# Encoder trunk on one core: in the differential attention, both distance products of a head before its score products, and the score products alternating between the two maps

## The chip, the cores and the metric

The kernel runs on one core of a Trainium2 chip. The metric is the device time of one execution in microseconds (us), the median of several runs. The other engines named below are TensorE (PE in the profile; its weight loads are listed apart as PEld), VectorE (DVE), ScalarE (ACT), GpSimd (POOL) and the queue that issues DMAs (SP).

## The reference, cut to what matters

Two layers of an encoder for 256 positions of width 1024. The part that the change touches is the attention with two score maps per head:

```
# q, k: (B,S,H,2,dh), H = 8 heads, 2 maps, dh = 64
sc = jnp.einsum('bqhcd,bkhcd->bhcqk', qi, k)
dist = jnp.abs(qpos[:, None] - kpos[None, :])
sc = sc - slopes[None, :, None, None, None] * dist
p = jax.nn.softmax(sc, axis=-1)
attn = p[:, :, 0] - lam * p[:, :, 1]
```

Each layer also has a cross-attention, a state-space branch, gates, three branch projections and a feed-forward part; the projections are the bulk of the work.

## The kernel before

All weights are streamed from memory in units of 128x1024 values into a ring of four slots. For each unit ScalarE rounds the raw values to a high part (`wH`, line 921) and VectorE or GpSimd takes the rest as a low part (`wL`, lines 1312 and 1240). TensorE multiplies by three products (high by high, high by low, low by high) into one of two large accumulators `PS`. `unit` (line 609 is the helper `mm` that issues each product) is the stream of the large products, 440 units for both layers.

Everything else is a side step, placed by hand between units by the table of `layer_plan`. On TensorE a step stands after the unit of its number; for head h of the differential attention the steps are `da_scores` (the products of this change), then `da_max` (VectorE, line 1484), `da_exp` (ScalarE, line 1071, which also writes the slope tile of head h+2, line 1009), `da_combine`, `da_turn`, `da_copy`, `da_values` and `da_head`, and `da_scores` of the next head comes three units after that of the one before it. There are 8 heads in each of 2 layers, so `da_scores` runs 16 times.

Map m of a head accumulates in its own bank, `S0` for map 0 and `S1` for map 1 (each 128x512: two blocks of 128 queries by 256 keys). First comes the distance product in bf16 (a diagonal tile of slopes by `dist`, 128 rows deep, 512 columns), then two fp32 score products, one for each block of queries, added onto it. A head has 64 dimensions in each map, and `qT` and `kT` (both in `regB`) hold map 0 in partitions 0 to 63 and map 1 in partitions 64 to 127, so a score product is 64 rows deep. `take(lay, m)` waits until bank m was released by its last reader (`side_free`). For heads 1 to 7 that is `da_exp` of the head before, whose second of four exponentials releases bank 0 and whose fourth bank 1.

Of the kernel before, what the change touches and what calls it, by code (L numbers as in the profile page):

```python
# [39 lines left out]
NT = T // P  # L40
# [3 lines left out]
HEADS, HALF = 8, 4  # L44
DH = 64
# [224 lines left out]
def build(nc, x, mem, mix_norm_g, w_in, lq1, lk1, lq2, lk2, subln_g, conv_w, conv_b, dt_bias, A_log, D_skip,  # L270
# [3 lines left out]
    with ctx:  # L274
# [3 lines left out]
        def sem(name):  # L278
            return ctx.enter_context(nc.semaphore(name))
# [138 lines left out]
        slope_ready = sem("slope_ready")  # L418
# [181 lines left out]
        def _(pe):  # L600
            side = [0, 0, 0, 0]

            def take(lay, bank):

                pe.wait_ge(side_free[bank], lay * side_uses[bank] + side[bank] + 1)
                side[bank] += 1

            def mm(o, l, r, first, last):
                return nc.tensor.matmul(o, l, r, start=first, stop=last, skip_group_check=True)  # L609
# [113 lines left out]
            def step(lay, kind, i):  # L723
# [48 lines left out]
                elif kind == "da_scores":  # L772
# [2 lines left out]
                        wait_evacuated(pe, lay, "k", half)  # L775
                    for m in range(2):
                        take(lay, m)
                        if m == 0:
                            pe.wait_ge(slope_ready, HEADS * lay + i + 1)
                        mm(S[m][:, :], slopes[:, P * (i % 2):P * (i % 2 + 1)], dist[:, :], True, False)  # L780
                        r = slice(DH * m, DH * (m + 1))
                        for t in range(NT):
                            ins = mm(S[m][:, T * t:T * (t + 1)], qT[half][r, j, P * t:P * (t + 1)],
                                     kT[half][r, j, :], False, True)
                    ins.then_inc(da_sc, 1)
# [28 lines left out]
                elif kind == "xs_turn":  # L814
                    bank = XS_BANK[i]
                    take(lay, bank)
                    n, t = i // 2 + 2, i % 2
# [77 lines left out]
            for lay in range(DEPTH):  # L895
                side[:] = setup_side
                each_step("pe", lambda u, g, c: unit(lay, u, g, c), lambda g: None, lambda *s: step(lay, *s),
                          lambda g: ffn_units(lay, g))
                counted = [n - m for n, m in zip(side, setup_side)]
# [840 lines left out]
```

## Time and profile before

| | |
|---|---|
| time, median of 3 runs | 1439.89 us (1439.86 to 1440.32) |
| span of the profiled execution, first to last instruction | 1438.7 us |
| TensorE busy | 1417.2 us, 99% of the span |
| VectorE / ScalarE / GpSimd busy | 65% / 61% / 23% |
| DMA, mean rate | 178 GB/s |
| granted TensorE clock, mean | 0.998 of full speed |

The profiled execution gives its span; its own time is not listed apart. The median is 1.2 us above the span, which is what lies around the first and the last instruction. Busy time says how long an engine had work in it, not whether the work was dense. An fp32 product appears as two matmul records with a weight load each, an fp32r or bf16 product as one. The record of the first distance product of a head is missing from the trace (16 of 32 are there), but its weight load is recorded.

### The profile page before, as it was taken

What the parts mean: (1) busy time and instruction counts of PE and PEld (TensorE: products, weight loads), DVE (VectorE), ACT (ScalarE), POOL (GpSimd) and SP (SyncE); (2) the same over time, 40 slices, a digit from 0 to 9 for tenths busy, and PEclk for the clock granted to TensorE, in tenths of its full rate; (3) what the DMA queues carried; (4) which work ended last, traced back from release to release, by engine and by line L of the source; (5) the groups of instructions that cost most, each with busy time, mean ns of one, the idle gap of its engine ahead of it and who ended that gap; (6) DMA issues with size and microseconds to landing.
All of it is one profiled execution on the core that took longest, in us unless ns stands there. A gap on an engine that the chain in (4) does not pass through costs nothing.

```text
span 1438.7 us, 25282 instructions
## 1 busy us (share of the span) xinstructions
PE 1417.2 (99%) x8861; PEld 1266.6 (88%) x8877; DVE 937.6 (65%) x1223; ACT 876.4 (61%) x1408; POOL 337.1 (23%) x161
## 2 busy tenths in 40 slices
PE   7999999999999999999999999999999999999997
PEld 7899888888888889998899998988888888999986
DVE  5478475787998446554444764668889875565543
ACT  7576667886755455445466665678777464544453
POOL 0410000010023344444423000001110244354442
PEclk9999999999999999999999999999999999999999
DMA  7655445475665655556555554454777556555664
GB/s 247 191 174 162 131 119 148 141 215 195 210 191 177 189 177 162 177 183 239 179 179 180 163 162 119 140 172 124 221 190 227 170 176 190 162 176 180 195 225 146
DMA packets 158496, 255.48 MB, mean 178 GB/s; under 512 B 12729, under 2 KB 58923, under 8 KB 158379
## 3 DMA queue, kind: packets, MB, share of 16 engines
q1 hardware_dynamic: 157819, 252.84, 57.4%
q8 instruction: 61, 1.00, 0.3%
q10 hardware_dynamic: 560, 1.18, 0.2%
q14 instruction: 56, 0.46, 0.1%
HBM read 252.80 MB, written 1.18 MB: 177 GB/s over the span
## 4 chain that ended last, share of the span: by engine, by line
PE 98%; ACT 1%; DVE 0%; DMA 0%; DVEq 0%; issue 0%; ACTq 0%; SPq 0%
PE PS L609 85%; PE S L609 9%; PE S L616 1%; PE S L820 0%; PE S L885 0%; PE S L791 0%; DMA regA<-in_mem_dram 0%; PE S L761 0%; PE S L811 0%; ACT regB L996 0%; DVE wL L1312 0%; DVEq L1388 0%; ACT hH L1003 0%; ACT wH L921 0%; ACTq L998 0%
## 5 line engine op out<-in xcount | busy, mean ns | idle before, releaser
L921 ACT CAST wH<-w_raw 128x1024 fp32r<-128x1024 f32 x443 | 457.5, 1042 | 427.2 <-PE PS L609 374.4
L1312 DVE TENSOR_TENSOR wL<-w_raw,wH 128x1024 fp32r<-128x1024 f32 (+1 forms) x331 | 459.5, 1393 | 355.3 <-ACT wH L921 333.8
L1240 POOL TENSOR_TENSOR wL<-w_raw,wH 128x1024 fp32r<-128x1024 f32 (+1 forms) x112 | 285.5, 2550 | 409.7 <-ACT wH L921 409.6
L609 PE MATMUL PS<-hH,wH 128*128 128x256 f32 (+1 forms) x1488 | 370.9, 287 | 0.0
L609 PE MATMUL PS<-hL,wH 128*128 128x256 f32 (+1 forms) x1488 | 365.2, 283 | 0.0
L609 PEld LDWEIGHTS PS<-hH,wH 128*128 128x128 f32 (+1 forms) x1488 | 283.9, 191 | 3.3 <-issue 2.7
L609 PEld LDWEIGHTS PS<-hL,wH 128*128 128x128 f32 (+1 forms) x1488 | 284.2, 191 | 0.6
L609 PE MATMUL PS<-wH,actH 128*128 128x512 f32 x560 | 223.9, 400 | 0.0
L609 PE MATMUL PS<-wH,actL 128*128 128x512 f32 x560 | 218.5, 390 | 0.0
L609 PE MATMUL PS<-hH,wL 128*128 128x256 f32 (+1 forms) x1488 | 211.0, 283 | 0.0
L609 PEld LDWEIGHTS PS<-hH,wL 128*128 128x128 f32 (+1 forms) x1488 | 192.0, 191 | 0.0
L609 PE MATMUL PS<-wH,hH 128*128 128x512 f32 x384 | 159.1, 414 | 0.0
L609 PE MATMUL PS<-wH,hL 128*128 128x512 f32 x384 | 150.4, 392 | 0.0
L609 PE MATMUL PS<-wL,actH 128*128 128x512 f32 x560 | 150.0, 390 | 0.0
L609 PEld LDWEIGHTS PS<-wL,actH 128*128 128x128 f32 x560 | 105.1, 188 | 22.4
L609 PEld LDWEIGHTS PS<-wH,actH 128*128 128x128 f32 x560 | 105.3, 188 | 22.2 <-issue 1.4
L609 PEld LDWEIGHTS PS<-wH,actL 128*128 128x128 f32 x560 | 105.3, 188 | 22.1 <-issue 1.4
L609 PE MATMUL PS<-wL,hH 128*128 128x512 f32 x384 | 103.2, 390 | 0.0
L609 PEld LDWEIGHTS PS<-wH,hH 128*128 128x128 f32 x384 | 72.2, 188 | 17.8 <-issue 4.6
L1267 POOL TENSOR_TENSOR scr<-actHf,dts 128x512 f32<-128x512 f32 x16 | 20.6, 1285 | 284.2 <-PE S L791 223.8
L609 PEld LDWEIGHTS PS<-wL,hH 128*128 128x128 f32 x384 | 72.1, 188 | 15.9
L609 PEld LDWEIGHTS PS<-wH,hL 128*128 128x128 f32 x384 | 72.3, 188 | 15.4 <-issue 1.9
(237 smaller groups left out, 1533.5 us busy)
## 6 DMA issues: line engine op xcount, KB each, us to landing
w_raw<-in_w_in_dram SPq DMA_DIRECT2D x192, 512.0 KB
w_raw<-in_w_ffn_in_dram SPq DMA_DIRECT2D x176, 256.0 KB
w_raw<-in_w_branch_dram SPq DMA_DIRECT2D x64, 512.0 KB
w_raw<-in_w_ffn_out_dram SPq DMA_DIRECT2D x44, 512.0 KB
w_raw<-in_w_mem_kv_dram SPq DMA_DIRECT2D x35, 512.0 KB
regA<-cs_rows SPq DMA_DIRECT2D x64, 256.0 KB, 4.7
w_raw<-in_w_out_dram SPq DMA_DIRECT2D x16, 512.0 KB
regA<-in_mem_dram SPq DMA_DIRECT2D x6, 512.0 KB, 4.8
```

Source lines behind the costliest of these rows:

```text
L609: return nc.tensor.matmul(o, l, r, start=first, stop=last, skip_group_check=True)
L616: ins = nc.tensor.transpose(dst[:, at:at + P], src(t, k), ident[:, :])
L921: nc.scalar.copy(wH[:, slot].rearrange("p k c -> p (k c)")[:, q], raw[:, slot].rearrange("p k c -> p (k c)")[:, q]).then_inc(h_done[slot], 1)
L1240: nc.gpsimd.tensor_tensor(wL[:, slot].rearrange("p k c -> p (k c)")[:, q], raw[:, slot].rearrange("p k c -> p (k c)")[:, q], wH[:, slot].r ...
L1267: nc.gpsimd.tensor_tensor(v3(xsd[i % 2], HPG), v3(xsN[g][:, c, :], HPG), dgain[:, SH * c + HPG * g:SH * c + HPG * (g + 1)].unsqueeze(2) .b ...
L1312: v.tensor_tensor(wL[:, slot].rearrange("p k c -> p (k c)")[:, q], raw[:, slot].rearrange("p k c -> p (k c)")[:, q], wH[:, slot].rearrange ...
```

## The change

Only `da_scores` changes. Both banks are taken first, then the slope tile is waited for; both distance products are issued one behind the other; then the four score products follow in the order block 0 of map 0, block 0 of map 1, block 1 of map 0, block 1 of map 1.

```
--- before
+++ after
                     for m in range(2):
                         take(lay, m)
-                        if m == 0:
-                            pe.wait_ge(slope_ready, HEADS * lay + i + 1)
+                    pe.wait_ge(slope_ready, HEADS * lay + i + 1)
+                    for m in range(2):
                         mm(S[m][:, :], slopes[:, P * (i % 2):P * (i % 2 + 1)], dist[:, :], True, False)
-                        r = slice(DH * m, DH * (m + 1))
-                        for t in range(NT):
+                    for t in range(NT):
+                        for m in range(2):
+                            r = slice(DH * m, DH * (m + 1))
                             ins = mm(S[m][:, T * t:T * (t + 1)], qT[half][r, j, P * t:P * (t + 1)],
                                      kT[half][r, j, :], False, True)
                     ins.then_inc(da_sc, 1)
```

The order of instructions on TensorE at head 0 of layer 0, before. `S0` and `S1` are the banks of the maps, `dist,slopes` is the distance product, `regB` a score product (two matmul records each), `PS0` the large accumulator:

```order
L609 MATMUL PS0<-wL,hH 128x512 x3
L609 MATMUL S0<-dist,slopes 128x512 [waits slope_ready,side_free0,psum_free1]
L609 MATMUL S0<-regB 128x256 x2
L609 MATMUL S1<-dist,slopes 128x512 [waits side_free1]
L609 MATMUL S1<-regB 128x256 x2
L609 MATMUL PS0<-wH,hH 128x512 [waits h_done1]
```

The same place in the changed kernel:

```order
L609 MATMUL PS0<-wL,hH 128x512 x3
L609 MATMUL S0<-dist,slopes 128x512 [waits side_free1,slope_ready,side_free0,psum_free1]
L609 MATMUL S1<-dist,slopes 128x512
L609 MATMUL S0<-regB 128x256
L609 MATMUL S1<-regB 128x256
L609 MATMUL S0<-regB 128x256
L609 MATMUL S1<-regB 128x256
L609 MATMUL PS0<-wH,hH 128x512 [waits h_done1]
```

The distance product of map 1 has moved ahead of the score products of map 0, its wait for `side_free1` has moved to the first distance product, and map 0 and map 1 now take turns. The number and the shapes of the products are the same.

Head 2 of layer 0 on TensorE, before, where the fp32 values product of another head stands directly ahead:

```order
L609 MATMUL S2<-regB,scr 128x128 x3
L609 MATMUL S0<-dist,slopes 128x512 [waits slope_ready,side_free0]
L609 MATMUL S0<-regB 128x256 x2
L609 MATMUL S1<-dist,slopes 128x512 [waits side_free1]
L609 MATMUL S1<-regB 128x256 x2
L609 MATMUL PS0<-hH,wH 128x256 [waits h_done3]
```

And in the changed kernel:

```order
L609 MATMUL S2<-regB,scr 128x128 x3
L609 MATMUL S0<-dist,slopes 128x512 [waits slope_ready,side_free1,side_free0]
L609 MATMUL S1<-dist,slopes 128x512
L609 MATMUL S0<-regB 128x256
L609 MATMUL S1<-regB 128x256
L609 MATMUL S0<-regB 128x256
L609 MATMUL S1<-regB 128x256
L609 MATMUL PS0<-hH,wH 128x256 [waits h_done3]
```

The neighbours on both sides are unchanged here too. The other engines keep their order.

## Rows read from the trace of the kernel before

**Rows 1.** The page: span, busy time, TensorE clock in 40 slices, chain that ended last.
```profile
span 1438.7 us, 25282 instructions
PE 1417.2 (99%) x8861; PEld 1266.6 (88%) x8877; DVE 937.6 (65%) x1223; ACT 876.4 (61%) x1408; POOL 337.1 (23%) x161
PEclk9999999999999999999999999999999999999999
PE 98%; ACT 1%; DVE 0%; DMA 0%; DVEq 0%; issue 0%; ACTq 0%; SPq 0%
```

**Rows 2.** The table of waits on TensorE, whole span.
```profile
engine line waited for: us in total, times, longest us
PE PS L629 <- DMA regB<-in_da_subln_g_dram: 7.6, 1, 7.6
PE S L616 <- DVEq L1388: 1.1, 2, 0.5
PE S L609 <- issue: 1.0, 6, 0.2
PE S L616 <- DVEq L1344: 1.0, 1, 1.0
PE PS L609 <- issue: 0.2, 1, 0.2
```

**Rows 3.** The timeline of head 0, layer 0, weight loads and matmuls.
```profile
start us, us, engine line op out<-in xcount [idle before <-releaser]
168.49 0.10 PEld L609 LDWEIGHTS S<-dist,slopes 128*128 128x128 bf16 x1 [0.26 <-issue]
168.81 1.13 PE L609 MATMUL S<-regB 64*128 64x256 f32 x4 [0.16 <-issue]
169.87 0.10 PEld L609 LDWEIGHTS S<-dist,slopes 128*128 128x128 bf16 x1 [0.33 <-issue]
170.19 1.13 PE L609 MATMUL S<-regB 64*128 64x256 f32 x4
171.25 0.19 PEld L609 LDWEIGHTS PS<-wH,hH 128*128 128x128 f32 x1 [0.33 <-issue]
171.35 0.19 PEld L609 LDWEIGHTS PS<-wH,hL 128*128 128x128 f32 x1
171.58 0.39 PE L609 MATMUL PS<-wH,hL 128*128 128x512 f32 x1
171.59 0.19 PEld L609 LDWEIGHTS PS<-wH,hH 128*128 128x128 f32 x1
171.81 0.39 PE L609 MATMUL PS<-wH,hH 128*128 128x512 f32 x1
171.82 0.19 PEld L609 LDWEIGHTS PS<-wH,hL 128*128 128x128 f32 x1
```

**Rows 4.** Durations of the score matmuls and of the distance products, all heads.
```profile
engine op xcount: duration ns min/median/max, first and last start us, forms
L609 PE MATMUL S<-regB x128: 376/376/480, 168.8 to 980.6; 64*128 64x256 f32 x128
L609 PEld LDWEIGHTS S<-dist,slopes x32: 95/96/100, 168.5 to 979.5; 128*128 128x128 bf16 x32
```

**Rows 5.** The timeline around the only other products 64 rows deep (line 828).
```profile
69.12 0.52 PE L609 MATMUL PS<-hH,wL 128*128 128x256 f32 x3
69.57 0.33 PE L828 MATMUL S<-ident,scr 64*128 64x64 f32 x2
70.06 0.28 PE L609 MATMUL PS<-hL,wH 128*128 128x256 f32 x1
70.17 0.28 PE L609 MATMUL PS<-hH,wH 128*128 128x256 f32 x1
```

**Rows 6.** The timeline of head 2: its first distance load directly behind a values product.
```profile
193.73 0.83 PE L609 MATMUL S<-regB,scr 128*128 128x128 f32 x6
194.29 0.10 PEld L609 LDWEIGHTS S<-dist,slopes 128*128 128x128 bf16 x1
194.71 1.13 PE L609 MATMUL S<-regB 64*128 64x256 f32 x4
```

**Rows 7.** The timeline ahead of head 5: last exponential of head 4, and the first distance load.
```profile
241.86 0.48 ACT L1071 ACTIVATE scr<-S,small 128x256 f32<-128x256 f32 x1
242.31 0.32 ACT L1009 ACTIVATE slopes<-ident 128x128 bf16<-128x128 f32 x1
243.60 0.10 PEld L609 LDWEIGHTS S<-dist,slopes 128*128 128x128 bf16 x1
```

**Rows 8.** Busy time of the engines in the two stretches that hold all heads.
```profile
core 0: us, PE busy (x) PEld busy (x) DVE busy (x) ACT busy (x) POOL busy (x), PEclk, DMA share, GB/s
168.00:280.00 112.00, 110.78 (x702) 95.79 (x709) 69.99 (x114) 76.39 (x178) 1.05 (x1) 1.00 0.49 142
876.00:988.00 112.00, 110.78 (x703) 95.89 (x710) 70.35 (x114) 76.61 (x179) 1.05 (x1) 1.00 0.48 142
```

**Rows 9.** The tables of waits of ScalarE, VectorE and the DMA queue, 160 to 280 us.
```profile
ACT wH L921 <- PE PS L609: 31.5, 14, 4.6
DVE wL L1312 <- ACT wH L921: 40.6, 20, 5.1
DVE small L1484 <- PE S L609: 2.9, 5, 0.9
SPq L532 <- DVE wL L1312: 87.7, 27, 5.5
```

## The prediction

> **What bounds the kernel now.** I read the page first, then the waits of TensorE, then single instructions around one head. The page shows TensorE busy for 1417.2 of 1438.7 us and 98% of the chain that ended last, with the clock at full speed (the 2.4 GHz level) in every slice [rows 1]. Busy could still hide gaps, so the waits come next: TensorE waits 7.6 us for the first DMA and after that 3.3 us in all, none of it at a distance or score product for another engine [rows 2]. The others wait for TensorE. In the first stretch with heads ScalarE's rounding waits 31.5 us for products to release ring slots, VectorE waits 40.6 us for the rounding, and the DMA queue 87.7 us for slots [rows 9]; VectorE is busy for 70 and ScalarE for 76 of 112 us [rows 8]. So a nanosecond taken out of TensorE's stream is a nanosecond of the kernel, until some step is late.
>
> **What a head costs now.** In head 0 the first distance load starts at 168.49, the score matmuls of map 0 at 168.81, the second distance load at 169.87, the score matmuls of map 1 at 170.19, and the next large product's load at 171.25 [rows 3]. So a map is a distance block of 0.32 and a score block of 1.06, and a head 2.76 us; 16 heads are 44 us, 3.1% of the span.
>
> The score block taken apart: four matmul records end 1.13 after their first start; the first lasts 0.480, the others 0.376 [rows 3, 4]. The 0.104 between them is a weight load that nothing hides. The last record starts 1.13 - 0.376 = 0.754 after the first, so the pitch is (0.754 - 0.104)/3 = 0.217. From the last start to the next load 1.06 - 0.754 = 0.306 pass: one pitch, and 0.089 in which nothing is issued. This is the crossing from products 64 rows deep to ones 128 rows deep. The distance block tells the other direction: 0.323 less 0.089 leaves 0.234, which is near the 0.23 between two large products of 512 columns (171.58, 171.81) [rows 3]. A third place with 64 rows confirms it: the three matmuls at 69.12 have a pitch of (0.52 - 0.28)/2 = 0.12 and would be through at 69.48, but the 64-row one starts at 69.57, 0.09 later [rows 5].
>
> **The change, part by part.**
>
> 1. *Crossings.* A head crosses four times now (128 to 64 and back, twice), afterwards twice. Removed are two idle pieces of 0.089 and one naked weight load of 0.104, the one behind the second crossing into 64 rows: 0.282 a head. Nothing else ran on TensorE in them, and nothing hides them. Over 16 heads 4.5 us.
>
> 2. *The second distance product behind the first.* The trace has no two bf16 products in a row. From below its load is hidden, and the block costs a pitch of about 0.213 (0.234 less the 0.02 that the load at 168.49 seems to cost), a gain of 0.02. From above the whole load record of 0.096 is naked [rows 4], 0.31 in place of 0.234, a loss of 0.07. In head 2 the bf16 load directly behind an fp32 product started at once, before that product was through [rows 6]. I take 0.234 as now, thus zero, and keep +0.3 and -1.2 us for the whole kernel as bounds.
>
> 3. *Alternating halves.* The eight score passes of a head (four products, two records each) now run A1 A2 B1 B2 A3 A4 B3 B4, A in partitions 0 to 63 and bank S0, B in 64 to 127 and bank S1. In series they cost 8 x 0.217 = 1.74. No row shows two neighbouring products in different halves, so I bound it from both sides. At best B1 runs beside A2, A3 beside B2 and B3 beside A4: five slots in place of eight, 3 x 0.217 = 0.65 a head, 10.4 us in all. At worst each of the three changes of half costs what a crossing costs with its naked load, 0.089 + 0.104 = 0.193, so 0.58 a head or 9.3 us lost.
> Between them I go by how weight loads stand to matmuls. Every load in the stream starts with the start of the matmul ahead of it and not sooner: 171.58 and 171.59, 171.81 and 171.82 [rows 3]. If that order holds when the half changes, the load of B1 starts with A2, takes 0.107 (its 0.104 and issue), and B1 then need not wait for A2 to end. B1 starts 0.107 after A2 in place of 0.217: 0.11 saved at each of three changes, 0.33 a head, 5.3 us in all. I take this value. It is nearest to the rows, which show loads in order and one matmul ahead, and it needs only that the halves can work at once. That they are treated as parts of their own is suggested by the idle 0.089 at every crossing, which equal shapes do not have.
> The Trainium skill (TensorE: Matmul & The Clock Gate, Part 3: Packing small matmuls) says that matmuls in different row groups run at the same time, with starts about 4 ns apart, and that weight loads are pulled ahead when the row group differs. By that rule the sum would take the whole 10.4 us of five slots; no row here shows it.
>
> 4. *The moved wait.* Bank 1 is now needed at the first distance product, 1.38 us earlier (169.87 less 168.49) [rows 3]. The closest head is head 5: the fourth exponential of head 4 ends at 241.86 + 0.48 = 242.34, and the head starts at 243.60 [rows 7]. 1.26 us are left, so the wait costs nothing; without that cover it would cost what it is late, with the whole large stream queued behind it. The units between two heads take as long as before, so this distance does not shrink with the change itself. The slope tile was written two heads ago.
>
> 5. *Who sees the end of the head.* The maxima on VectorE wait for the last score product (2.9 us in 5 waits [rows 9]) and simply start sooner. Nothing is added on any other engine or queue.
>
> The sum: 4.5 + 0 + 5.3 + 0 = 9.8 us. The profiled span is 1438.7, and 1.2 us lie around it; against the median of 1439.89 this gives 1430.1 us, 0.7% faster.
>
> **The rivals.**
>
> - *Full overlap of the halves.* Loads may run two matmuls ahead when their half is free. For it speaks that the gap between loads is long enough (0.107 of each 0.217); against it that no load in the rows ever starts that early. 4.5 + 10.4 = 14.9 us, 1425.0 us.
> - *No overlap: the change does not do what it says.* The passes stay in line at 0.217 and only the crossings are saved: 1435.4 us. For it speaks that every row has matmuls at the pitch of their columns, with 64 rows or with 128.
> - *A change of half costs like a crossing.* Three of 0.193 against 0.282 saved make a head 0.30 longer, 4.8 us in all: 1444.7 us. It decides from 0.094 a change, and is measurable from about 0.15. For it speaks that the engine does go idle when the depth changes, against it that the depth here stays at 64.
> - *The gain is taken back.* A weight unit or a side step becomes late when TensorE is 0.6 us faster per head: 1438 to 1440 us. Against it speak the waits of all others for TensorE [rows 8, 9].
>
> **How the numbers follow.** Half overlap 0.36, full overlap 0.27, no overlap 0.22, change of half as dear as a crossing 0.07, taken back 0.05, and 0.03 for something outside. The predicted time is that of the first, 1430.1. The range takes in the first three with the bounds of item 2: from 1424.5 to 1436.2; within the likeliest case alone it would be 1429 to 1432. A measurement of this kernel can tell about 0.2%, 2.9 us, from no change; even the case without overlap lies 4.5 us below. Faster 0.88, same 0.05, slower 0.07.
>
> **What would show it.** Between the first distance load of a head and the next large load: 2.15 us for my case, 1.83 for full overlap, 2.48 for none, 3.06 if a change of half costs like a crossing, where 2.76 stand now. The score records should be eight in one block, with one first record of 0.48. In my case the starts inside the block would alternate between steps of 0.22 and of 0.11; in the rival of full overlap some starts would be nearly together. The idle 0.089 should be there 32 times in place of 64. I would be wrong if ScalarE's last exponential stood directly ahead of a head, if TensorE showed waits on rounding in these stretches, or if the second distance block came out far from 0.23.

## The result and the profile after

The changed kernel takes 1424.21 us (1424.01 to 1424.59), against 1439.99 us for the kernel before in the same rounds: a ratio of 0.989, 95% interval 0.988 to 0.990, 15.8 us less. The time lies 0.3 us under the low end of the forecast range and 5.9 us under the predicted 1430.1. It was clearly faster, but by 15.8 us where 9.8 were forecast.

The page of the changed kernel, lines of the span, the busy times and the chain that ended last:

```profile
span 1422.9 us, 25302 instructions
PE 1402.7 (99%) x8877; PEld 1256.5 (88%) x8877; DVE 936.0 (66%) x1223; ACT 876.6 (62%) x1408; POOL 337.8 (24%) x161
PE 91%; ACT 3%; DVE 2%; DVEq 1%; issue 1%; ACTq 1%; DMA 0%; SPq 0%
```

The span is 15.8 us shorter than in [rows 1]. TensorE's share of the chain fell from 98% to 91%; ScalarE and VectorE now have a part in it. The first is where the gain came from, the second is where some of it went.

The timeline of head 0 of layer 0 after the change, weight loads and matmuls:

```profile
168.61 0.12 PEld L609 LDWEIGHTS S<-dist,slopes 128*128 128x128 bf16 x2 [0.26 <-issue]
168.61 0.60 PE L609 MATMUL S<-dist,slopes 128*128 128x512 bf16 x2
169.15 0.73 PEld L609 LDWEIGHTS S<-regB 64*128 64x128 f32 x8 [0.42 <-issue]
169.15 1.13 PE L609 MATMUL S<-regB 64*128 64x256 f32 x8
170.21 0.50 PE L609 MATMUL PS<-wH,hH 128*128 128x512 f32 x1
```

Eight score matmuls take 1.13 us, exactly what four took in [rows 3]. A head is 170.21 - 168.61 = 1.60 us where it was 2.76. A head behind a values product gains the same: head 2 takes 1.69 us where it took 2.85 (before, its first distance load is at 194.29 and the next large load at 197.14; after, they are at 192.11 and 193.80). The start of the block seen through a narrow window, for both kinds of record:

```profile
169.15 0.19 PEld L609 LDWEIGHTS S<-regB 64*128 64x128 f32 x2 [0.42 <-issue]
169.15 0.49 PE L609 MATMUL S<-regB 64*128 64x256 f32 x2
```

Two matmuls, and two loads, start within 0.01 us of each other: one record lasts 0.480, the pair covers 0.49. A window up to 169.60 holds four:

```profile
169.15 0.70 PE L609 MATMUL S<-regB 64*128 64x256 f32 x4
```

So both passes of map 0 have a pass of map 1 beside them. It is not the second pass of one product beside the first of the next, as I had counted.

From the table of waits of TensorE in the changed kernel, the first DMA and the two lines that are new against [rows 2]:

```profile
PE PS L629 <- DMA regB<-in_da_subln_g_dram: 7.5, 1, 7.5
PE S L792 <- DVEq L1499: 0.8, 2, 0.4
PE S L609 <- ACT scr L1072: 0.6, 2, 0.3
```

The new ones are two places, once in each layer. Each is longer for the weight loads than for the matmuls, which run on for a while. The first place in layer 0, the weight load of a state-space product that writes bank `S0`, and the exponentials ahead of it:

```profile
246.26 0.47 ACT L1072 ACTIVATE scr<-S,small 128x256 f32<-128x256 f32 x1
246.86 0.19 PEld L609 LDWEIGHTS S<-regA 128*128 128x128 f32 x1 [0.54 <-ACT scr L1072]
```

The same two in the kernel before:

```profile
251.86 0.47 ACT L1071 ACTIVATE scr<-S,small 128x256 f32<-128x256 f32 x1
252.97 0.30 PEld L609 LDWEIGHTS S<-regA 128*128 128x128 f32 x2
```

The step is `cb` of group 0, which takes bank 0 after the exponentials of head 5. The second of them releases it. Before, it ended at 252.33, 0.64 us ahead of the load; now it ends at 246.73, the load follows 0.13 later, and TensorE's weight loads had stood still for half a microsecond (its matmuls for 0.30). The second place is the transposes of head 7:

```profile
277.74 0.88 DVE L1497 SCALAR_TENSOR_TENSOR scr<-scr,small 128x256 f32<-128x256 f32 x2
278.76 0.31 PEld L792 LDWEIGHTS S<-ident,scr 128*128 128x128 f32 x3 [0.80 <-issue]
```

They need what VectorE combines until 278.62. In the kernel before, the combination ended at 285.19 and the load came at 286.41, so there 1.22 us were in hand:

```profile
284.31 0.88 DVE L1496 SCALAR_TENSOR_TENSOR scr<-scr,small 128x256 f32<-128x256 f32 x2
286.41 0.14 PEld L791 LDWEIGHTS S<-ident,scr 128*128 128x128 f32 x1
```

### The profile page after: what moved, and what is told of

The parts are those of the page before. It is cut to its first block, busy times and chain, and to the rows that moved or that the text cites. A ratio compares the mean times of both kernels' runs of the same rounds, so it can differ in the third digit from the quotient of the medians.

```text
span 1422.9 us, 25302 instructions
## 1 busy us (share of the span) xinstructions
PE 1402.7 (99%) x8877; PEld 1256.5 (88%) x8877; DVE 936.0 (66%) x1223; ACT 876.6 (62%) x1408; POOL 337.8 (24%) x161
## 4 chain that ended last, share of the span: by engine, by line
PE 91%; ACT 3%; DVE 2%; DVEq 1%; issue 1%; ACTq 1%; DMA 0%; SPq 0%
PE PS L609 81%; PE S L609 7%; PE S L616 1%; DVE wL L1313 1%; ACT wH L922 1%; ACT scr L1072 1%; PE S L821 0%; PE S L886 0%; PE S L792 0%; DMA regA<-in_mem_dram 0%; DVEq L1486 0%; DVE actLf L1522 0%; ACT actLf L947 0%; PE S L761 0%; DVEq L1524 0%
## 5 line engine op out<-in xcount | busy, mean ns | idle before, releaser
L609 PEld LDWEIGHTS PS<-wL,hH 128*128 128x128 f32 x384 | 72.1, 188 | 15.8
```

## The experiments

The theory after the result: products in different halves of the rows run side by side in full, weight loads included, and this alone is most of the gain; the crossings are the rest; two late chains on VectorE took some back. Open were four things: whether the halves or something else did it, whether the alternation matters, how far a product may overtake, and whether the pauses can go.

### Both maps from one half

```
                             for m in range(2):
-                                r = slice(DH * m, DH * (m + 1))
+                                r = slice(0, DH)
```

> The order of the changed kernel, but both maps take their scores from the lower half of the partitions, so map 1 gets the scores of map 0 (the second map is not computed). If the different halves are what lets the products run together, the eight passes stand in line again: a head of 1.60 + 4 x 0.216 = 2.47 us, the kernel near 1435.3 us, and this is what the saved crossings alone are worth (4.6 us). If alternating banks alone did it, 1424 us as with the change.

Measured: 1435.22 us (1434.80 to 1435.82), ratio 0.997 (0.996 to 0.998). The timeline of its head 0:

```profile
167.79 0.12 PEld L609 LDWEIGHTS S<-dist,slopes 128*128 128x128 bf16 x2 [0.26 <-issue]
168.33 1.99 PE L609 MATMUL S<-regB 64*128 64x256 f32 x8
170.25 0.50 PE L609 MATMUL PS<-wH,hH 128*128 128x512 f32 x1
```

Shapes, banks and order are those of the change, and the eight matmuls take 1.99 us in place of 1.13. The head is 2.46. So it is the half of the rows that lets them run together, and alternating banks do nothing by themselves. The run also gives the worth of the other part of the change, the two crossings saved and the second distance product behind the first: 2.76 - 2.46 = 0.30 a head, 4.8 us in all, and the time is 4.74 us under that of the kernel before.

### Four crossings kept, one pair together

```
-                    for m in range(2):
-                        mm(S[m][:, :], slopes[:, P * (i % 2):P * (i % 2 + 1)], dist[:, :], True, False)
-                    for t in range(NT):
-                        for m in range(2):
+                    for what in ("d0", "00", "d1", "01", "10", "11"):
+                        if what[0] == "d":
+                            m = int(what[1])
+                            mm(S[m][:, :], slopes[:, P * (i % 2):P * (i % 2 + 1)], dist[:, :], True, False)
+                        else:
+                            m, t = int(what[0]), int(what[1])
                             r = slice(DH * m, DH * (m + 1))
```

> All four crossings kept: distance 0, one score product of map 0, distance 1, then the second of map 0, the first and the second of map 1. Overlap theory, in order: one pair runs together, two slots of 0.217 fewer than before, a head 2.33 us in place of 2.76, the kernel 1439.9 - 6.8 = 1433 us. If the gain came from having the distance products together, nothing: 1439.9 us.

Measured: 1433.16 us (1433.00 to 1434.12), ratio 0.995 (0.994 to 0.997), 6.80 us less. Its head 0:

```profile
168.32 0.70 PE L609 MATMUL S<-regB 64*128 64x256 f32 x2 [0.16 <-issue]
168.95 0.39 PE L609 MATMUL S<-dist,slopes 128*128 128x512 bf16 x1
169.27 1.13 PE L609 MATMUL S<-regB 64*128 64x256 f32 x6
```

Ahead of the second distance product two matmuls run alone; behind it six take the time of four. The two score products of map 1 stand behind that distance product, and the first score product of map 0 did not get one of them beside it. A distance product over all 128 rows acts as a barrier: nothing ran beside it, and no score product behind it was seen to pass it. This run alone does not show the second part, because in it two waiting products (distance 1 and the second of map 0) stand ahead of map 1, and two are not passed in any run (see below). The kernel before shows it: there only the distance product stands between the maps, and the scores of map 1 start behind it, at 170.19 [rows 3]. This is why the kernel before had no overlap at all. One rival stays open: in all these runs the distance product of map 1 writes the same bank as the scores of map 1, so no run tells whether its depth or its bank holds them back.

### The maps one after the other

```
-                    for t in range(NT):
-                        for m in range(2):
+                    for m in range(2):
+                        for t in range(NT):
```

> Both distance products first, but the score products in the old order (both blocks of map 0, then both of map 1). Theory 'in order, one product per half': a whole fp32 product (two passes) is issued when its half is free and the product ahead of it has been issued. Then only the second product of map 0 and the first of map 1 run together, six slots of 0.216 in place of four: a head from its first distance load to the next large load is 1.60 + 2 x 0.216 = 2.03 us, the kernel about 1429 us. Rival 'a queue for each half, any later product may overtake': four slots, 1.60 us, 1424 us. Rival 'no overlap unless they alternate': eight slots, 2.47 us, 1435.3 us.

Measured: 1424.08 us (1423.88 to 1424.31), ratio 0.989 (0.987 to 0.991), the same as the change. The in-order theory, for which I had 1429, falls. The rival has the right time; whether really any later product may overtake is the next question. A narrow window at the start of its score block:

```profile
168.47 0.20 PEld L609 LDWEIGHTS S<-regB 64*128 64x128 f32 x2 [0.42 <-issue]
168.47 0.49 PE L609 MATMUL S<-regB 64*128 64x256 f32 x2
```

Map 1 starts with map 0, though both products of map 0 stand ahead of it in the program. The alternation, half of the change, is worth nothing here. What matters is that no 128-row product stands between the maps: against the kernel before, this run only has the second distance product ahead of the scores of map 0.

### How far a product overtakes

Each score product is cut into two of 128 columns, so that each map has four, once map by map and once in turn.

```
-                    for t in range(NT):
-                        for m in range(2):
-                            r = slice(DH * m, DH * (m + 1))
-                            ins = mm(S[m][:, T * t:T * (t + 1)], qT[half][r, j, P * t:P * (t + 1)],
-                                     kT[half][r, j, :], False, True)
+                    for m in range(2):
+                        for t in range(NT):
+                            for k in range(2):
+                                r = slice(DH * m, DH * (m + 1))
+                                ins = mm(S[m][:, T * t + P * k:T * t + P * (k + 1)],
+                                         qT[half][r, j, P * t:P * (t + 1)],
+                                         kT[half][r, j, P * k:P * (k + 1)], False, True)
```

> The changed kernel with the score products map by map, and each cut into two of 128 columns: four products of map 0 stand ahead of the first of map 1. If the halves have queues that reach over all of them, map 1 still starts within some 20 ns of map 0, and a head is 1.6 to 1.8 us (eight passes of a half at a pitch of 0.11, with the loads at their limit of 0.107, instead of four of 0.216): 1424 to 1427 us. If only two products can be overtaken, map 1 starts two products, 0.44 us, later: a head of 2.05 us and more, 1431 us or more.

Measured: 1430.42 us (1430.35 to 1431.09), ratio 0.993 (0.992 to 0.995). A head takes 2.18 us. This is near the second case and far from the first: map 1 starts 0.55 us behind map 0 (168.15 and 168.70 in the rows below), where that case had 0.44.

```
-                    for m in range(2):
-                        for t in range(NT):
-                            for k in range(2):
+                    for t in range(NT):
+                        for k in range(2):
+                            for m in range(2):
```

> The products of 128 columns of e8_quarters, with the maps in turn. Theory: a half takes one product that runs and one that waits, and a product that finds its half full holds up everything behind it. With the maps in turn map 1 is then never held up: its first load comes within some 10 ns of that of map 0, and a head falls from 2.18 to 2.18 - 0.55 = 1.63 us if the loads of both halves can run side by side; the kernel 1424 to 1425 us. Rival: what made e8_quarters long is that weight loads of 0.107 in both halves share one path and 16 of them do not fit (16 x 0.107 = 1.7 us): a head stays at about 2.2 us and the kernel at 1430 us.

Measured: 1424.21 us (1423.85 to 1424.73), ratio 0.989 (0.987 to 0.991), a head 1.63 us, as the theory had it. The score blocks of head 0, first map by map, with a window that ends 0.54 us behind the start and one that begins right after it, then the whole block:

```profile
168.15 0.71 PE L609 MATMUL S<-regB 64*128 64x128 f32 x4
168.59 0.30 PEld L609 LDWEIGHTS S<-regB 64*128 64x128 f32 x3
168.15 1.71 PE L609 MATMUL S<-regB 64*128 64x128 f32 x16
```

And the maps in turn, a window that ends 0.53 us behind the start, then the whole block, matmuls and loads:

```profile
168.56 0.71 PE L609 MATMUL S<-regB 64*128 64x128 f32 x8
168.56 1.16 PE L609 MATMUL S<-regB 64*128 64x128 f32 x16
168.55 0.97 PEld L609 LDWEIGHTS S<-regB 64*128 64x128 f32 x16 [0.42 <-issue]
```

With the maps in turn twice as many matmuls start in the first half microsecond. Map by map only map 0 runs until 168.70, where two loads start at once (the row of three loads spans 0.30, one of them at 168.59 and the two others 0.19 before its end). By then four passes, two products, of map 0 have been issued; the third starts and the fourth waits. What is counted is products, not work: here one waiting product of 128 columns is overtaken and two are not, while with the maps one after the other a single one of 256 columns, which takes as long as these two, was overtaken. My reading is that a half holds one product that runs and one that waits, and that a product that finds its half full holds up all behind it, the other half's too. The runs fit it, but they would fit as well a rule that TensorE looks past one waiting product, whichever half it is for. In the changed kernel each map has just two products, which is why the order was free. The rival of a shared path for the loads is out: a naked load takes 0.10 (171.25 to 171.35 in [rows 3]), 16 of them in a line would be 1.6 us, and here all 16 loads lie within 0.97.

### The two pauses

Steps of VectorE moved in the table of `layer_plan`: the maxima of head 5 one unit earlier, ahead of other work that waited in VectorE's order, and the convolutions of block 2 one unit later, behind the combination of head 7. The other numbers in the second edit fall by one so that the steps behind the convolutions stay where they were.

```
-        put(u + 1, "dve", "da_max", h)
+        put(u if h == 5 else u + 1, "dve", "da_max", h)
...
-        u = first("xbc", b) + {4: 4, 5: 4, 0: 5, 1: 5, 2: 7, 3: 4}[b]
+        u = first("xbc", b) + {4: 4, 5: 4, 0: 5, 1: 5, 2: 8, 3: 4}[b]
-        put(u + {4: 6, 5: 5, 0: 3, 1: 5, 2: 6, 3: 6}[b], "act", "conv_silu", n)
+        put(u + {4: 6, 5: 5, 0: 3, 1: 5, 2: 5, 3: 6}[b], "act", "conv_silu", n)
-                at = u + {0: [7, 7], 1: [7, 6], 2: [9, 11], 3: [8, 10]}[b][t]
+                at = u + {0: [7, 7], 1: [7, 6], 2: [8, 10], 3: [8, 10]}[b][t]
```

> The changed kernel with two groups of VectorE steps moved in the hand-written table: the maxima of head 5 one unit earlier (ahead of the state-space gain and of the next split), and the convolutions of block 2 one unit later (behind the combination of head 7). Theory: the two new pauses of TensorE in each layer (0.57 and 0.60 us) come from these two chains being late; then they go and the kernel takes about 1421.9 us. Rival: the pauses come from something else, or only move to the next step: 1424.2 us or a little less.

Measured: 1421.66 us (1421.54 to 1421.73), ratio 0.987 (0.986 to 0.989). Both waits are gone from its table of waits on TensorE, of which this is all but the first DMA:

```profile
PE S L616 <- DVEq L1389: 1.1, 2, 0.5
PE S L616 <- DVEq L1345: 0.9, 1, 0.9
PE PS L609 <- ACT wH L922: 0.2, 1, 0.2
```

The same move in the kernel before the change:

> The kernel before with the two groups of VectorE steps moved as in e3_steps_moved, and nothing else. Theory: before the change these steps were in time, by a few tenths of a us, so moving them gives nothing: 1439.9 us, within 0.5. Rival: the move is a gain of its own, some 2.5 us: 1437.5 us.

Measured: 1439.90 us (1439.31 to 1440.41), ratio 1.000 (0.999 to 1.001). The steps were in time there; the 2.5 us that the move gains in the changed kernel are part of what the change brought and did not deliver. One move at a time:

> The changed kernel with only the maxima of head 5 moved one unit earlier. Theory: the pause of 0.57 us ahead of the first B-by-C product of the state-space branch goes in each layer, the one ahead of the transposes of head 7 stays: 1.2 us less, 1423.0 us. Rival: the time saved at the first place is lost at the second, which stays late on its own clock: 1424.2 us.

Measured: 1421.76 us (1421.59 to 1422.36). I had expected 1423.0: this one move takes away nearly all of both pauses. The load ahead of which TensorE stood for half a microsecond now stands free, and the exponential that releases its bank ends at 244.09 + 0.47 = 244.56:

```profile
244.09 0.47 ACT L1072 ACTIVATE scr<-S,small 128x256 f32<-128x256 f32 x1
245.37 0.73 PEld L609 LDWEIGHTS S<-regA 128*128 128x128 f32 x4
```

The second pause shrinks too: the weight loads of the transposes of head 7 had an idle 0.80 before them in the changed kernel, and here, from the table of waits of the weight loads between 160 and 290 us:

```profile
PEld S L792 <- issue: 0.3, 1, 0.3
```

The traces show that the lateness is older than head 7. VectorE's work from the split ahead of head 7 to the end of its combination takes 16.0 us in the changed kernel (262.58 to 278.62) and 16.2 here (260.44 to 276.68). But it starts 0.57 us ahead of head 7's first distance load there, and 1.22 us ahead here, 0.65 sooner. First the changed kernel, then this one:

```profile
262.58 1.23 DVE L1313 TENSOR_TENSOR wL<-w_raw,wH 128x1024 fp32r<-128x1024 f32 x1 [2.49 <-ACT wH L922]
263.15 0.10 PEld L609 LDWEIGHTS S<-dist,slopes 128*128 128x128 bf16 x1
```

```profile
260.44 1.23 DVE L1313 TENSOR_TENSOR wL<-w_raw,wH 128x1024 fp32r<-128x1024 f32 x1 [2.50 <-ACT wH L922]
261.66 0.10 PEld L609 LDWEIGHTS S<-dist,slopes 128*128 128x128 bf16 x1
```

How the delay passes from head 5 to this split, step by step, is not followed here.

> The changed kernel with only the convolutions of block 2 moved one unit later. Theory: the pause of 0.60 us ahead of the transposes of head 7 goes in each layer, the other stays: 1423.0 us. Rival: no change, 1424.2 us.

Measured: 1422.86 us (1422.57 to 1423.49), as expected: the second pause goes, the first stays (its table of waits still has 0.6 us for `ACT scr L1072`). The kernel with both moves has the lowest median of the study, 18.3 us under the kernel before; the 0.10 us between it and the kernel with the maxima alone lie within the scatter of the runs.

## Why the prediction was right or wrong

*What bounds the kernel* was right. The time went down with TensorE's stream, and the two chains that became late are the only exceptions.

*Item 1, the crossings*, and *item 2, the second distance product*, were right: together 0.282 a head forecast, 0.30 measured with both maps in one half, 4.8 us in place of 4.5. The two distance matmuls last 0.60 where one lasts 0.38 to 0.39, so the second costs about 0.22. It was taken at 0.234, with a gain of 0.02 as its bound, and that is the 0.02 by which the two items together came out better.

*Item 3, the alternating halves*, is the step that failed, twice. First, I let the load of B1 start only with A2, because every load in the rows starts with the matmul ahead of it. Those rows could not tell this, because in all of them both belong to the same rows of the array; in different halves the two loads start 0.01 us apart. Second, I laid the passes out as one line A1 A2 B1 B2, so that even the best case had five slots. Each half runs its own line: four slots. The bound of 0.65 a head was therefore no bound; measured are 2.46 - 1.60 = 0.86 a head, 13.8 us in all against the 5.3 taken and the 10.4 of the bound. The rival of full overlap had the mechanism, with a chance of 0.27, and it too was mis-sized: 14.9 us, where 18.3 are measured without the pauses. That its 1425.0 lies within 1 us of the result is luck: the 3.4 us that it left out and the 2.5 of the pauses, which it did not have, nearly cancel. The rule of the Trainium skill (TensorE: Matmul & The Clock Gate, Part 3: Packing small matmuls) was nearer than my reading of the rows. It says that weight loads and matmuls of different row groups overlap, and the trace agrees, with starts within 0.01 us.
The same page says matmuls start in strict order. The run map by map shows map 1 starting beside the first product of map 0, with a second product of map 0 ahead of it in the program and not yet running; on this the measurement decides. For the order across halves the page's rule does not hold here.

*Item 4, the moved wait*, was right for what it looked at, the next head's first distance product: at head 5 the 1.26 us in hand are still there, 236.74 to 238.00.

```profile
236.26 0.48 ACT L1072 ACTIVATE scr<-S,small 128x256 f32<-128x256 f32 x1
238.00 0.11 PEld L609 LDWEIGHTS S<-dist,slopes 128*128 128x128 bf16 x2
```

It was blind to the rest, and so was *item 5*, which looked only at who waits for TensorE at the end of a head. A step of TensorE whose inputs run on VectorE's own clock comes nearer when TensorE gains over a microsecond per head. Head 5 starts 5.60 us earlier than before (243.60, 238.00), and the exponential that releases bank 0 for `cb` of group 0 ends 5.60 earlier too (252.33, 246.73). TensorE's way from the start of head 5 to `cb` is 1.16 shorter by head 5 itself. `cb` had 0.64 us in hand, less the 0.13 that it needs after the release, so it is 0.65 late; the idle time shown before its load is 0.54. In the rivals this was "the gain is taken back", dismissed by the totals of busy and waiting time. These totals can't show a chain that is late once in a layer.

*The range* does not follow from its own terms: the 1425.0 and 1435.4 of the rivals with the bounds of item 2 give 1424.7 to 1436.6, and not 1424.5 to 1436.2. The result lies outside either.

*The sum in its terms*: 16 heads by 1.16 us are 18.6 us. With the pauses removed, 18.3 us are measured. The pauses take 2.5 of it, and 15.8 remain.

*What would show it*: the forecast said that starts nearly together would mean full overlap, and a head of 1.83. They are together, and the head is 1.60.

## What to carry to other kernels

Products 64 rows deep run side by side when they lie in different halves of the partitions and nothing over all rows stands between them (here each half also had a bank of its own; one bank for both was not tried). Put the full-depth products of both ahead, which also saves a crossing each way. With more than two products to a half, let the halves take turns. When the engine that bounds the kernel gets faster, look at each step that waits for another engine in the stretch and how much it has in hand, above all those on banks that the faster work shares.

## What the runs showed of the hardware

- fp32 score products 64 rows deep in the two halves of the array: eight matmul records in 1.13 us, as four before; all in one half, 1.99 us.
- A change of depth between 128 and 64 rows leaves TensorE without work for 0.089 us and, ahead of an fp32 product, exposes its weight load of 0.10 us; a pair of such changes saved, with the two distance products brought together, is worth 0.30 us.
- Products of the other half overtake one waiting product (two passes in fp32), not two: with four products in a row to a half, the other half began 0.55 us later.
- Weight loads of the two halves run side by side: 16 loads of 0.10 each lie within 0.97 us.
